# Rotating q through two PSUM banks, k inside the products of v, and a weight split moved behind both

## The chip, the cores and the metric

One Trainium2 chip, one of its cores. The metric is the device time of one launch in microseconds, of which three runs were made of the kernel before: 2287.13, 2292.32 and 2295.41 us, median 2292.32 us. One further execution was recorded by the profiler; everything read from a trace here comes from that one.

## The reference

Two layers of a block for a latent sequence of 512 tokens and a context of 256 tokens, width 1024. Layer 0 mixes with a state-space scan and a long convolution; layer 1 mixes with windowed attention over the latent tokens and the whole context. Each layer has a gated feed-forward network (hidden width 2816). All is float32. The part that the change touches is the start of the attention of layer 1:

```
p = h @ w_qkv                       # q: 16 heads, k and v: 4 heads, 64 wide each
q_l, k_l = axial_rope(q_l), axial_rope(k_l)     # latent tokens only
# per block of 128 queries: scores against 384 neighbours and 256 context keys,
# softmax with a sink, times v; then the output projection
```

`axial_rope` turns each head's columns in pairs: the result is `t * cos + R(t) * sin`, where R swaps the two halves of a group of 32 columns and negates one of them.

## The kernel before, in words

Activations lie transposed, features on the 128 partitions and tokens along the free axis: 768 columns, of which the first 512 are latent. Precision is kept by splitting each operand of a product into a high part and a low part (float32 rounded by a copy, and the rest by a subtraction). Each product is then three matmuls: high weights times high activations, low weights times high, high weights times low (`tiles`, L513, L514, L518).

Weights come in "jobs", each up to 2 x 8 tiles of 128 x 128, in a ring of three slots that SP fills by DMA. A job has two halves, b = 0 and 1. The high part of a half is made by VectorE (`split_high`, L1604, a CAST of 128 x 1024) into `WH`, which has one buffer for each half, and the low part by GpSimd (`low`, L2121) in place. So the split of the next job's half can only begin when TensorE is through with this job's half: `next_high(gs, i, b)` waits on the semaphore `blocks_done` for that. TensorE waits on `w_lo` ahead of each half.

The attention's projections are six jobs, written out in order: jobs 0 to 3 are the eight 128-wide blocks of q (512 columns each), job 4 the two blocks of k (768 columns), job 5 is v (tokens on the partitions: six groups of 24 matmuls of 256 columns, L1052 to L1054; its results lie in PSUM banks 4, 5 and 7, groups 4 and 5 in bank 7). Blocks of q and k accumulate in banks 0 to 3; ScalarE copies each into `T[:, b, :]` (L1473).

The rotation R is one more matmul by a constant matrix, in plain float32 (`rotated(b, n)`, L1036; each makes two records in the trace), from `T[:, b]` into PSUM bank 6. VectorE then makes, for block m, the product of that bank with the sines (L2013), the product of `T[:, b]` with the cosines (L2014) and their sum (L2016), and signals `q_done`. For k (m = 8, 9) it writes the result out into `KD` with four instructions (L2022) and signals `k_done`.

The order on TensorE: block 0 of job n, then the rotations of both blocks of job n - 1, then block 1 of job n. The second of the two rotations waits for `q_done` of the first, because both use bank 6. Both k rotations stand behind v. The order on VectorE: ahead of block m = 2j the splits of both halves for job j + 1, each as `blocks_done` allows; at m = 8 also the splits for the first job of the output projection (`AT["qkv"] + 5` is v, the splits are for the job behind it), which wait for v's last matmuls. Then the ten blocks' arithmetic in order, then `NSINK` (L2027).

Behind that stands the attention itself: scores on TensorE (L1077), which wait for `k_done` and `v_done`; row maxima on VectorE (L2040); exponentials on ScalarE (L1489), with a table load ahead of the first, which also wait for a small copy on GpSimd (L2302) that stands in GpSimd's order behind its splits for the output projection and waits for `NSINK`; transpositions on TensorE (L1089).

Of the kernel before, what the change touches and what calls it, by code (L numbers as in the profile page):

```python
# [7 lines left out]
LAT, CTX = 512, 256  # L8
# [33 lines left out]
IDENT, ONES, KGTJ, KLTJ, LE, GE, ROT = range(7)  # L42


def weight_jobs():

    jobs, at = [], {}

    def stage(name, items):
        at[name] = len(jobs)  # L50
        jobs.extend(items)

    ada0 = [("ada", 0, n) for n in range(24)]
    ada1 = [("ada", 1, n) for n in range(24)]
    stage("ada_a", ada0[:8] + ada1[:8])
    stage("uv", [j for n in range(8) for j in (("uv", 0, n), ada0[8 + 2 * n], ada0[9 + 2 * n])])
    stage("x0", [j for n in range(4) for j in (("x0", 0, n), ada1[8 + 2 * n], ada1[9 + 2 * n])])
    stage("z", [j for n in range(4) for j in (("z", 0, n), ada1[16 + 2 * n], ada1[17 + 2 * n])])
    stage("xbc", [("xbc", 0, n) for n in range(6)])
    stage("out0", [("halves", 0, ((0, 1), (1, 1))), ("halves", 0, ((2, 1), (0, 0))), ("halves", 0, ((1, 0), (2, 0)))])  # L60
    stage("out0b", [("out0", 0, n) for n in range(3, 8)])
    for layer in range(2):
        if layer:
            stage("qkv", [("q", 0, n) for n in range(4)] + [("k", 0, 0), ("v", 0, 0)])
            stage("out1", [("out1", 0, n) for n in range(4)])
        for half in range(2):
            stage(f"up{layer}{half}", [("up", layer, half * FH + n) for n in range(FH)])
            stage(f"down{layer}{half}", [("down", layer, (half, n)) for n in range(8)])
    return jobs, at


JOBS, AT = weight_jobs()
# [90 lines left out]
def build_kernel(nc, A, out):  # L163
    f32 = mybir.dt.float32
    f32r = mybir.dt.float32r
    ALU = mybir.AluOpType
# [3 lines left out]
    with ctx:  # L170
        def sb(name, shape):
            return ctx.enter_context(nc.sbuf_tensor(name, shape, f32))
# [12 lines left out]
        C = sb("consts", [P, 7, P])  # L185
# [36 lines left out]
        T = Tt[:, :].rearrange("p (k t) -> p k t", k=4)  # L222

        def region(at, *dims):

            n = 1
            for d in dims:
                n *= d
            names = "abcd"[:len(dims)]
            ap = R[:, at:at + n]  # L230
            if len(dims) == 1:
                return ap
            return ap.rearrange(f"p ({' '.join(names)}) -> p {' '.join(names)}",
                                **{names[i]: dims[i] for i in range(1, len(dims))})
# [49 lines left out]
        RC = region(8704, 2, LAT)  # L284
# [28 lines left out]
        PS = ctx.enter_context(nc.psum_tensor("psum", [P, 8, 512], f32))  # L313
# [56 lines left out]
        def read(gs, i, b, eng):  # L370

            eng.wait_ge(pair_free[PLAN[gs[0]][b][0]], along([PLAN[g][b][1] + 1 for g in gs], i))
# [115 lines left out]
        def _(pe):  # L488
            mm = pe.matmul

            def half_ready(gs, i, b):
                if JOBS[gs[0]][0] == "ada":
                    pe.wait_ge(w_loaded[gs[0] % SLOTS][b], along([16 * (g // SLOTS + 1) for g in gs], i))
                else:
                    pe.wait_ge(w_lo, along([2 * NTH[g] + b + 1 for g in gs], i))
# [150 lines left out]
            for c in range(2):  # L646

                for t in range(6):
                    n = 6 * c + t
# [27 lines left out]
                for m in range(6):  # L677
                    j, f = 1 - m // 3, m % 3
                    n = 6 * c + m
# [8 lines left out]
                    for odd in range(2):  # L688
                        ts = (2 * odd, 2 * odd + 1) if f < 2 else (4 + odd,)
                        for t in ts:  # L690
                            o = (t * 256 + f * P) if f < 2 else (1024 + (t - 4) * P)
                            ins = mm(PS[:, 2 * (n % 2) + odd, :], C3[:, j, o:o + P], SD[:, j, t, :],  # L692
                                     start=t == ts[0], stop=t == ts[-1])
# [120 lines left out]
            for k in range(KT):  # L814
                for w, moved in ((WDH, HNH0), (WDL, HNH0), (WDH, HNL)):
                    for a, b in SEGS:
                        ins = mm(TP[0:32, a:b], w[:, k, :], moved[:, k, a:b],
                                 start=k == 0 and w is WDH and moved is HNH0, stop=k == KT - 1 and moved is HNL)
            ins.then_inc(dt_mm, 1)
            pe.wait_ge(dt_rows, 1)  # L820
            for t in range(6):
                ins = mm(PS[:, 4, 32 * t:32 * t + 32], T[0:32, 0, t * P:t * P + P], C[0:32, IDENT, 0:32],
                         start=True, stop=True)
# [16 lines left out]
            for n in range(6):  # L840
# [3 lines left out]
                if n == 5:  # L844
# [3 lines left out]
                    for t in range(6):  # L848
                        for q in range(2):
                            ins = mm(NP[32 * q:32 * q + 32, t * P:t * P + P], NAC[:, 32 * t:32 * t + 32], C[:, IDENT, :],  # L850
                                     start=True, stop=True)
# [179 lines left out]
            def rotated(b, n):  # L1031

                read([AT["qkv"] + n // 2], 0, b, pe)
                if n:
                    pe.wait_ge(q_done, n)
                mm(PS[:, 6, :], C[:, ROT, :], T[:, b, 0:LAT], start=True, stop=True).then_inc(q_rot, 1)  # L1036

            for n in range(5):
                two_blocks([AT["qkv"] + n], 0, parts, LS if n < 4 else SEGS,
# [3 lines left out]
            g = AT["qkv"] + 5  # L1043
            half_ready([g], 0, 1)

            for t in range(6):
                acc = PSF[:, 2048 + 256 * t:2048 + 256 * t + 256] if t < 4 else PS[:, 7, 256 * (t - 4):256 * (t - 3)]
                for k in range(KT):
                    wh = WH[:, k // 4, 2 * (k % 4):2 * (k % 4) + 2, :].rearrange("p a b -> p (a b)")
                    wl = WL[:, g % SLOTS, 2 * k:2 * k + 2, :].rearrange("p a b -> p (a b)")  # L1050
                    h, l = HNH[:, k, t * P:t * P + P], HNL[:, k, t * P:t * P + P]
                    mm(acc, h, wh, start=k == 0, stop=False)  # L1052
                    prev = mm(acc, h, wl, start=False, stop=False)
                    ins = mm(acc, l, wh, start=False, stop=k == KT - 1)  # L1054

            prev.then_inc(blocks_done, 1)
            ins.then_inc(blocks_done, 1)
            for b in range(2):
                rotated(b, 8 + b)


            pe.wait_ge(k_done, 2)
            pe.wait_ge(v_done, 2)
# [471 lines left out]
        def _(dve):  # L1535
            ch = Count(dve, v_ch)
            TS, TT, STT = dve.tensor_scalar, dve.tensor_tensor, dve.scalar_tensor_tensor
# [12 lines left out]
            for layer in range(3):  # L1550
                dve.wait_ge(mlp_arg, layer + 1)
                n = 64 if layer < 2 else P
                h, q = HF[layer][0:n, :, :], halves(T[0:n, 0, :], 2)
# [52 lines left out]
            for c in range(2):  # L1606
                for t in range(6):
                    n = 6 * c + t
# [20 lines left out]
                for m in range(6):  # L1629
# [13 lines left out]
                    n = 6 * c + m  # L1643
# [46 lines left out]
            def next_high(gs, i, b):  # L1690

                if gs[-1] + 1 < len(JOBS):
                    dve.wait_ge(blocks_done, along([2 * g + 1 + b for g in gs], i))
                    split_high([SPLIT[NTH[g] + 1] for g in gs], i, b)
# [309 lines left out]
            for m in range(10):  # L2004
                b = m % 2
                if b == 0:
                    for h in range(2):
                        next_high([AT["qkv"] + m // 2], 0, h)
                    if m == 8:
                        for h in range(2):  # L2010
                            next_high([AT["qkv"] + 5], 0, h)
                dve.wait_ge(q_rot, m + 1)
                TT(T[:, 2, 0:LAT], PS[:, 6, :], RC[:, 1, :], ALU.mult)  # L2013
                ch.link(TT(T[:, 3, 0:LAT], T[:, b, 0:LAT], RC[:, 0, :], ALU.mult))  # L2014
                dst = QT[:, m, :] if m < 8 else T[:, b, 0:LAT]
                TT(dst, T[:, 3, 0:LAT], T[:, 2, 0:LAT], ALU.add).then_inc(q_done, 1)  # L2016
                dve.wait_ge(q_done, m + 1)
                if m >= 8:

                    for g in range(2):  # L2020
                        for half in range(2):
                            ins = TS(KD[64 * half:64 * half + 64, 2 * b + g, :],  # L2022
                                     T[64 * g:64 * g + 64, b, :], -1.0, None, ALU.mult)
                    ins.then_inc(k_done, 1)

            dve.wait_ge(v_in, 16)
            TS(NSINK, vec("sink", 0, 16), -1.0, None, ALU.mult).then_inc(at_nsink, 1)  # L2027
# [453 lines left out]
```

## Time and profile before

| | |
|---|---|
| median of three runs | 2292.32 us (2287.13 to 2295.41) |
| profiled execution, its time | 2295.2 us |
| its span, first to last instruction | 2293.4 us |
| mean granted TensorE clock | 0.957 of full speed |
| TensorE matmuls | busy 2127.0 us, 93% of the span, 11802 instructions |
| VectorE | 866.7 us, 38% |
| ScalarE | 439.4 us, 19% |
| GpSimd | 821.3 us, 36% |
| DMA | 182.29 MB, mean 79 GB/s |

"Busy" is the sum of an engine's instruction times. PE is TensorE, PEld its weight loads, DVE VectorE, ACT ScalarE, POOL GpSimd. The granted clock is 1.00 at 2.4 GHz and 0.50 at 1.2 GHz; a value between is a mean over a stretch. The projections of the attention run from about 1578 us to 1697 us of the span, the attention itself from 1711 us to 1844 us.

### The profile page before, as it was taken

What the parts mean: (1) busy time and instruction counts of PE and PEld (TensorE: products, weight loads), DVE (VectorE), ACT (ScalarE), POOL (GpSimd) and SP (SyncE); (2) the same over time, 40 slices, a digit from 0 to 9 for tenths busy, and PEclk for the clock granted to TensorE, in tenths of its full rate; (3) what the DMA queues carried; (4) which work ended last, traced back from release to release, by engine and by line L of the source; (5) the groups of instructions that cost most, each with busy time, mean ns of one, the idle gap of its engine ahead of it and who ended that gap; (6) DMA issues with size and microseconds to landing.
All of it is one profiled execution on the core that took longest, in us unless ns stands there. A gap on an engine that the chain in (4) does not pass through costs nothing.

```text
span 2293.4 us, 29807 instructions
## 1 busy us (share of the span) xinstructions
PE 2127.0 (93%) x11802; PEld 1693.1 (74%) x11802; DVE 866.7 (38%) x1249; ACT 439.4 (19%) x826; POOL 821.3 (36%) x442
## 2 busy tenths in 40 slices
PE   6989988999989978989999999997879998999997
PEld 2468656887877767878888888885656677888886
DVE  4533544302337764241221121233236663322334
ACT  2331110001345541031000011002016612100110
POOL 1443536112227755242222222224210034444442
PEclk9999999999989989989999999998979998999998
DMA  9524323333110011111111211122110021223322
GB/s 340 189 88 165 110 101 112 122 130 115 61 55 2 1 38 57 64 46 65 61 48 63 77 65 62 44 69 75 56 36 1 1 69 65 94 82 105 100 74 73
DMA packets 50838, 182.29 MB, mean 79 GB/s; under 512 B 5680, under 2 KB 5936, under 8 KB 49712
## 3 DMA queue, kind: packets, MB, share of 16 engines
q1 hardware_dynamic: 49296, 171.53, 22.2%
q10 hardware_dynamic: 928, 6.36, 0.8%
q0 software_dynamic: 512, 2.95, 0.4%
q8 instruction: 75, 1.23, 0.2%
q14 instruction: 27, 0.22, 0.0%
HBM read 178.72 MB, written 2.10 MB: 79 GB/s over the span
## 4 chain that ended last, share of the span: by engine, by line
PE 86%; DVE 6%; POOL 3%; ACT 2%; DMA 1%; issue 1%; ACTq 0%; DVEq 0%; SPq 0%
PE psum L513 21%; PE psum L518 21%; PE psum L514 21%; PE psum L1089 2%; PE psum L1077 2%; PE psum L1106 2%; PE psum L692 1%; PE psum L728 1%; PE psum L580 1%; PE psum L655 1%; PE psum L907 1%; POOL weights_lo L2121 1%; PE psum L932 1%; PE psum L536 1%; PE psum L542 1%
## 5 line engine op out<-in xcount | busy, mean ns | idle before, releaser
L2121 POOL TENSOR_TENSOR weights_lo<-weights,weights_hi 128x1024 fp32r<-128x1024 f32 (+1 forms) x232 | 515.1, 2221 | 1034.9 <-DVE weights_hi L1604 1034.9
L1604 DVE CAST weights_hi<-weights 128x1024 fp32r<-128x1024 f32 (+1 forms) x232 | 165.0, 713 | 921.6 <-PE psum L518 751.9
L518 PE MATMUL psum<-normed_lo,weights_hi 128*128 128x512 f32 x1760 | 511.6, 354 | 0.0
L513 PE MATMUL psum<-normed_hi,weights_hi 128*128 128x512 f32 x1088 | 394.8, 363 | 8.4 <-POOL weights_lo L2121 8.4
L514 PE MATMUL psum<-normed_hi,weights_lo 128*128 128x512 f32 x1088 | 376.7, 361 | 0.0
L518 PEld LDWEIGHTS psum<-normed_lo,weights_hi 128*128 128x128 f32 x1760 | 287.2, 191 | 16.8
L513 PEld LDWEIGHTS psum<-normed_hi,weights_hi 128*128 128x128 f32 x1088 | 206.8, 190 | 57.6 <-POOL weights_lo L2121 6.2
L513 PE MATMUL psum<-normed_first_hi,weights_hi 128*128 128x512 f32 (+1 forms) x672 | 234.9, 350 | 13.1 <-POOL weights_lo L2121 12.6
L514 PEld LDWEIGHTS psum<-normed_hi,weights_lo 128*128 128x128 f32 x1088 | 207.7, 191 | 35.5 <-issue 1.2
L514 PE MATMUL psum<-normed_first_hi,weights_lo 128*128 128x512 f32 (+1 forms) x672 | 215.5, 342 | 0.0
L513 PE MATMUL psum<-hidden_hi,weights_hi 128*128 128x512 f32 (+1 forms) x528 | 189.2, 358 | 0.0
L514 PE MATMUL psum<-hidden_hi,weights_lo 128*128 128x512 f32 (+1 forms) x528 | 179.0, 354 | 0.0
L513 PEld LDWEIGHTS psum<-normed_first_hi,weights_hi 128*128 128x128 f32 x672 | 129.3, 192 | 49.7 <-POOL weights_lo L2121 14.6
L518 PE MATMUL psum<-hidden_lo,weights_hi 128*128 128x512 f32 (+1 forms) x528 | 160.5, 358 | 0.0
L514 PEld LDWEIGHTS psum<-normed_first_hi,weights_lo 128*128 128x128 f32 x672 | 129.3, 192 | 16.5 <-issue 1.2
L513 PEld LDWEIGHTS psum<-hidden_hi,weights_hi 128*128 128x128 f32 x528 | 99.1, 188 | 23.4
L514 PEld LDWEIGHTS psum<-hidden_hi,weights_lo 128*128 128x128 f32 x528 | 99.6, 189 | 14.9
L1705 DVE SCALAR_TENSOR_TENSOR temps<-psum,vectors,temps 128x511 f32<-128x511 f32 x112 | 63.8, 612 | 102.6 <-ACT temps L1260 101.6
L1450 ACT ACTIVATE temps<-psum 128x768 f32<-128x768 f32 (+1 forms) x44 | 31.1, 707 | 360.2 <-PE psum L518 355.7
L1454 ACT ACTIVATE hidden_hi<-temps 128x768 f32 (+3 forms) x44 | 32.5, 740 | 334.2 <-DVE temps L1987 334.2
L518 PEld LDWEIGHTS psum<-hidden_lo,weights_hi 128*128 128x128 f32 x528 | 87.1, 188 | 8.9
L513 PE MATMUL psum<-mixed_hi,weights_hi 128*128 128x512 f32 x224 | 77.7, 347 | 8.5 <-POOL weights_lo L2121 8.5
(306 smaller groups left out, 2981.7 us busy)
## 6 DMA issues: line engine op xcount, KB each, us to landing
weights<-in_wall SPq DMA_DIRECT2D x264, 512.0 KB, 4.0
weights<-in_wall SPq DMA_DIRECT2D x32, 384.0 KB, 3.2
weights<-in_wall SPq DMA_DIRECT2D x32, 320.0 KB, 3.1
residual<-in_xT SPq DMA_DIRECT2D x1, 3072.0 KB, 15.4
residual<-in_xT ACTq DMA_DIRECT2D x1, 3072.0 KB, 11.2
phase<-in_tab ACTq DMA_DIRECT2D x2, 1280.0 KB, 5.5
out_T<-normed SPq DMA_DIRECT2D x2, 1024.0 KB, 4.3
normed<-in_window SPq DMA_DIRECT2D x1, 1536.0 KB, 8.7
```

Source lines behind the costliest of these rows:

```text
L513: mm(acc[:, lo:hi], WH[:, b, k, :], high[:, lo:hi], start=st, stop=False)
L514: mm(acc[:, lo:hi], WL[:, s, HALF * b + k, :], high[:, lo:hi], start=False, stop=False)
L518: ins = mm(acc[:, lo:hi], WH[:, b, k, :], low[:, lo:hi], start=False, stop=en)
L536: mm(accs[b][:, lo:hi], WH[:, b, k, :], high[:, lo:hi], start=k == 0, stop=False)
L1077: ins = mm(PSF[:, 1024 * e + at0:1024 * e + at1], QT[rows, 2 * g + j, b * P:b * P + P], KD[rows, g, key:key + at1 - at0], start=c in (0, 2 ...
L1089: ins = pe.transpose(PSF[:, 2048 + t * P:2048 + t * P + P], EX[:, n % 4, 1 + t * P:1 + t * P + P], C[:, IDENT, :])
L1106: ins = mm(PS[64 * e:64 * e + 64, 6, 0:256].rearrange("p (j c) -> p j c", j=2), VT[:, kt, 64 * g:64 * g + 64], heads_e, start=t == 0, stop ...
L1450: run(T[:, 0, lo:hi], pair(0)[:, lo:hi], ACT.Silu).then_inc(pair_free[0], 1)
L1454: run(at_row(HIDH, r)[:, lo:hi], T[:, 1, lo:hi], ACT.Copy).then_inc(hid_hi, 1)
L1604: dve.tensor_copy(WH[:, b, 0:n, :], W[:, s, HALF * b:HALF * b + n, :]).then_inc(w_hi, 1)
L1705: ins = STT(t[:, a:e], p[:, a + shift:e + shift], w, t[:, a:e], ALU.mult, ALU.add)
L2121: TT(WL[:, s, at, :], W[:, s, at, :], WH[:, b, 0:width(gs[0], b), :].bitcast(f32), ALU.subtract).then_inc(w_lo, 1)
```

## The change

Rotations of q (n < 8) go to bank 6 for b = 0 and to bank 7 for b = 1, and rotation n waits for `q_done` n - 1, that is for the block two before it. TensorE waits for `q_done` 8 ahead of v, which writes bank 7. The rotations of k are issued inside v, behind its second and its fourth group of 24 matmuls, and use bank 6. VectorE's two splits for the first job of the output projection move from ahead of block 8's arithmetic to behind block 9's.

```diff
@@ rotated(b, n), TensorE
-                if n:
-                    pe.wait_ge(q_done, n)
-                mm(PS[:, 6, :], C[:, ROT, :], T[:, b, 0:LAT], start=True, stop=True).then_inc(q_rot, 1)
+                if n > 1:
+                    pe.wait_ge(q_done, n - 1 if n < 8 else n)
+                mm(PS[:, 6 + (b if n < 8 else 0), :], C[:, ROT, :], T[:, b, 0:LAT], start=True, stop=True) \
+                    .then_inc(q_rot, 1)
@@ products of v, TensorE
+            pe.wait_ge(q_done, 8)
             for t in range(6):
...
                     ins = mm(acc, l, wh, start=False, stop=k == KT - 1)
+                if t in (1, 3):
+
+                    rotated(t // 2, 8 + t // 2)
 
             prev.then_inc(blocks_done, 1)
             ins.then_inc(blocks_done, 1)
-            for b in range(2):
-                rotated(b, 8 + b)
@@ rotation arithmetic, VectorE
                     for h in range(2):
                         next_high([AT["qkv"] + m // 2], 0, h)
-                    if m == 8:
-                        for h in range(2):
-                            next_high([AT["qkv"] + 5], 0, h)
                 dve.wait_ge(q_rot, m + 1)
-                TT(T[:, 2, 0:LAT], PS[:, 6, :], RC[:, 1, :], ALU.mult)
+                TT(T[:, 2, 0:LAT], PS[:, 6 + (b if m < 8 else 0), :], RC[:, 1, :], ALU.mult)
...
                     ins.then_inc(k_done, 1)
+            for h in range(2):
+                next_high([AT["qkv"] + 5], 0, h)
```

## Rows read from the trace of the kernel before

**Rows 1.** Page, part 4: the chain that ended last, by engine.
```profile
PE 86%; DVE 6%; POOL 3%; ACT 2%; DMA 1%; issue 1%; ACTq 0%; DVEq 0%; SPq 0%
```

**Rows 2.** Waits, 1600 to 1715 us: us in total, times, longest.
```profile
PE psum L1036 <- DVE phase L2016: 8.8, 4, 2.2
```

**Rows 3.** Timeline of TensorE: start us, us, instruction [idle before <-releaser].
```profile
1626.07 1.02 PE L1036 MATMUL psum<-temps,consts 128*128 128x512 f32 x2
...
1637.33 0.40 PE L513 MATMUL psum<-normed_hi,weights_hi 128*128 128x512 f32 x1
...
1642.91 1.02 PE L1036 MATMUL psum<-temps,consts 128*128 128x512 f32 x2
...
1652.64 0.47 PE L513 MATMUL psum<-normed_hi,weights_hi 128*128 128x512 f32 x1
...
1661.08 1.02 PE L1036 MATMUL psum<-temps,consts 128*128 128x512 f32 x2
1664.30 1.52 PE L1036 MATMUL psum<-temps,consts 128*128 128x512 f32 x2 [2.20 <-DVE phase L2016]
...
1678.58 0.58 PE L1052 MATMUL psum<-weights_hi,normed_hi 128*128 128x256 f32 x1 [3.20 <-POOL weights_lo L2121]
```

**Rows 4.** Timelines of VectorE and GpSimd, beside the rotations from 1642.91 us on.
```profile
1643.96 0.69 DVE L2013 TENSOR_TENSOR temps<-psum,phase 128x512 f32<-128x512 f32 x1 [5.74 <-PE psum L1036]
...
1647.33 0.69 DVE L2013 TENSOR_TENSOR temps<-psum,phase 128x512 f32<-128x512 f32 x1 [1.35 <-PE psum L1036]
...
1650.15 2.40 POOL L2121 TENSOR_TENSOR weights_lo<-weights,weights_hi 128x1024 fp32r<-128x1024 f32 x1 [9.45 <-DVE weights_hi L1604]
...
1675.41 0.69 DVE L1604 CAST weights_hi<-weights 128x1024 fp32r<-128x1024 f32 x1 [6.74 <-PE psum L518]
```

**Rows 5.** Chain in order of time: start us, us, what.
```profile
1609.38 0.87 PE psum L1036 x2
```

**Rows 6.** Windows behind waits of TensorE (columns: stretch, length, busy by engine, PEclk, DMA) and two waits.
```profile
1612.40:1617.00 4.60, 4.57 (x12) 3.30 (x13) 2.67 (x4) 0.57 (x1) 0.54 (x1) 0.63 0.03 12
1646.10:1652.60 6.50, 6.47 (x26) 4.82 (x26) 2.67 (x4) 0.57 (x1) 2.40 (x1) 1.00 0.03 11
1026.10:1029.00 2.90, 2.90 (x17) 2.55 (x18) 1.99 (x3) 0.85 (x1) 2.40 (x1) 1.00 0.50 172
1917.30:1921.00 3.70, 3.63 (x9) 2.90 (x10) 2.81 (x3) 0.63 (x1) 2.38 (x1) 0.54 0.41 145
...
1026.06 0.50 PE L513 MATMUL psum<-normed_hi,weights_hi 128*128 128x512 f32 x1 [1.23 <-POOL weights_lo L2121]
...
1917.37 0.77 PE L513 MATMUL psum<-normed_hi,weights_hi 128*128 128x512 f32 x1 [1.91 <-POOL weights_lo L2121]
```

**Rows 7.** Timeline of all engines, end of v to the first transposition.
```profile
1697.21 1.30 DVE L1604 CAST weights_hi<-weights 128x1024 fp32r<-128x1024 f32 x2 [21.10 <-PE psum L1053]
...
1697.98 5.47 POOL L2121 TENSOR_TENSOR weights_lo<-weights,weights_hi 128x1024 fp32r<-128x1024 f32 x2 [19.45 <-DVE weights_hi L1604]
1698.24 0.59 ACT L1479 ACTIVATE phase<-psum 128x512 f32<-128x512 f32 x1
...
1701.29 2.71 DVE L2016 TENSOR_TENSOR temps<-temps 128x512 f32<-128x512 f32 x1
1704.03 2.26 DVE L2022 TENSOR_SCALAR phase<-temps 64x768 f32<-64x768 f32 x4
...
1710.69 2.08 PE L1077 MATMUL psum<-phase 64*128 64x256 f32 x8 [4.50 <-DVE phase L2022]
1710.90 0.19 POOL L2302 COPY phase<-phase 128x4 f32<-128x4 f32 x1 [7.46 <-DVE phase L2027]
1711.17 1.28 ACT L1489 ACT_TABLE_LOAD   x1 [12.33 <-POOL phase L2302]
...
1713.74 0.73 ACT L1489 ACTIVATE phase<-phase 128x513 f32<-128x513 f32 x1 [1.29 <-DVE phase L2040]
...
1716.44 1.11 PE L1089 MATMUL psum<-consts,phase 128*128 128x128 f32 x4
```

## Prediction

> **What bounds the kernel now.** I read the chain that ended last first: 86% of it is TensorE and 6% VectorE [rows 1], so time can only be won where TensorE stands still or runs at its low clock. The waits of the projection stage come next. TensorE stood 8.8 us in front of the rotation matmul, in four waits of 2.2 us each, always for the sum on VectorE [rows 2]. The timelines show the rest: 3.2 us ahead of v for the low part of its weights [rows 3], and from the end of v at 1697.21 us to the first scores at 1710.69 us a stretch of 13.5 us with only the two k rotations on TensorE [rows 7]. The change aims at the four waits and at the long stretch.
>
> **Part 1: two banks for q.** The reader is to follow one period, from one first rotation (time A) to the next. In the third period A is 1642.91 us. The arithmetic of the first block starts at 1643.96, that of the second only at 1647.33 after 1.35 us of idle, then comes the cast, then GpSimd's split from 1650.15 for 2.40 us, and TensorE's next block starts at 1652.64: 9.73 us after A [rows 3, 4]. With bank 7 the second rotation is issued right behind the first. A rotation takes 0.87 us [rows 5], so it ends at A + 1.74, before VectorE is through with the first block (A + 3.1, since the second would have started 1.35 us earlier than A + 4.42). VectorE's idle 1.35 us goes, nearly all of it (I take 1.32), and everything behind it moves up: the next block starts at A + 8.41.
>
> That is not when TensorE is ready. A full block of q takes 1642.91 - 1637.33 = 5.58 us [rows 3], so TensorE is through with two rotations and its block at A + 1.74 + 5.58 = 7.32, and now waits 1.1 us for the split. What is late next is thus the chain of arithmetic, cast and split, and a period is 8.41 + 5.58 = 13.99 us.
>
> - The second period of before lasted 1642.91 - 1626.07 = 16.84 us [rows 3], the first alike (1609.2 to 1626.07). They were longer than the chain asks because the clock fell after the 2.2 us wait: 0.63 in the window behind it [rows 6]. Gain 2.85 us each, 5.7 us.
> - The third kept its clock (1.00 [rows 6]) and was already bound by the split. Gain 9.73 - 8.41 = 1.3 us.
> - The fourth runs from 1661.08 to the end of k's second block, about 1675.2 (0.2 us ahead of the cast it releases at 1675.41 [rows 4]): 14.1 us. k's block takes 1661.08 - 1652.64 = 8.44 us [rows 3], so the new one is 1.74 + 8.44 = 10.2 us. VectorE and GpSimd are done with their part by A + 8.3 and are covered. Gain 3.9 us.
>
> Together 10.9 us. The 3.2 us ahead of v stay: its second half is still cast and split only when k's second block ends. The new wait for `q_done` 8 costs nothing: block 7's sum ends at about A + 5.1, five microseconds before k's second block. The new wait of a rotation for the block two before it has most of a period to spare. Bank 7 holds nothing else then.
>
> **Part 2: k inside v.** v becomes longer by two rotations. No row shows a rotation between matmuls of v; the nearest rows bound one between 0.87 us [rows 5] and 1.52 us at a falling clock [rows 3]. I take 0.87, as v is at full clock by its second group, so 1.7 us are lost. The second rotation waits for the first block's sum. Between them lie 48 matmuls at 18.6 / 144 = 0.13 us (1678.58 to 1697.21 [rows 3, 7]), 6.2 us, and the arithmetic needs 3.1 us, so there is no wait. Behind the second rotation 48 more matmuls follow, 5.6 us or more, plus its own 0.87; VectorE needs 3.1 us and the four writes into `KD`, 2.26 us [rows 7], 5.4 us in all. So `k_done` comes about 1 us ahead of the end of v. If that margin fails, it costs the overrun alone, as v's copies on ScalarE take 1.6 us beyond the end anyway.
>
> **Part 3: the split behind that.** Call the end of v E (1697.21 before). Before, VectorE first made the two casts, and then its sums met GpSimd's splits: the sum at L2016 took 2.71 us [rows 7], where a whole block's three operations otherwise fit into 2 us (A + 1.05 to A + 3.1 above). All this was on the path, 13.5 us to the scores. After, the casts still start at E, since they wait for v, but no k arithmetic follows them. TensorE waits for ScalarE's second copy, which ends at 1698.24 + 0.59, E + 1.6 [rows 7]; the scores start there.
>
> The gain isn't the whole 11.9 us. The exponentials wait for GpSimd's small copy, and this stands behind its two splits. Those start at E + 0.77 and took 5.47 us with VectorE's sums beside them; the split alone takes 2.40 us [rows 4], two 4.8. I take 5.1, because the second cast still overlaps. The copy then ends at E + 6.1, the table load (1.28 us) at E + 7.5, and the first exponential and its sum need 0.9 us [rows 7]; the first transposition starts at E + 8.4. Before, it started at 1716.44, E + 19.2 [rows 7]. Gain 10.8 us. Row maxima and the second pair of scores are ready by then (they took 5.7 us from the first score to that transposition, now E + 7.4), and behind it the order of work is the old one.
>
> The Trainium skill, "SBUF — State Buffer", section "Who interferes with whom", says that a VectorE instruction with two inputs in SBUF shuts GpSimd's reading instructions out or is shut out, whole instructions at a time, and that `tensor_scalar` can be in a mode that does the same. The stretched L2016 agrees. The row maxima have one input in PSUM; the little `NSINK` instruction is a `tensor_scalar`, and gives the rival "lock" below.
>
> **Sum.** 10.9 - 1.7 + 10.8 = 20.0 us off the profiled time of 2295.2 us: 2275.2 us. The median of the runs shown is 2.9 us below the profiled execution (2292.3), so for a median I say 2292.3 - 20.0 = 2272.3 us.
>
> **Rivals.**
> - *The clock falls after the new short waits.* Each 1.1 us wait for the split could do what 2.2 us did in three of four cases. For it: a wait of 1.91 us was followed by 0.54. Against it: 1.23 us by 1.00, and the third 2.2 us wait also by 1.00 [rows 6]. Price of one fall: in the fourth period of before, from the second rotation (1664.30) to the end of k's block (1675.2) went 10.9 us, where 0.87 + 8.44 = 9.3 would do [rows 3], so 1.6 us. Three such waits make 4.8 us: 2277 us. The Trainium skill, "TensorE: Matmul & The Clock Gate", section "A second HAM failure mode: psum-queue depth-cycling", says that cycling through PSUM banks with small pauses makes the clock swing and costs throughput. That is this rival; the trace is on neither side clearly.
> - *Lock.* `NSINK` on VectorE is queued behind the casts and ahead of the row maxima. If it waits until both splits are done (E + 5.9), the maxima follow at E + 6.1, the second pair of scores behind the first of them at E + 7.2, and the transposition 2.7 us later (as from 1713.74 to 1716.44 before [rows 7]) at E + 9.9: 1.5 us lost, 2274 us. Nothing in the rows shows an instruction of 16 columns so held.
> - *The clock is up when the attention starts.* TensorE now pauses 1.6 us instead of 13.5, and might start the attention at its high clock, where the first scores took 2.08 us and the four transpositions 1.11 [rows 7], both at the low one. But it is gated by the exponentials until E + 8.4; at most some 6 us behind that, half paced before, shrink by 3 us (an estimate): 2269 us.
> - *The change doesn't take the stretch away*, because k's arithmetic ends late after all, say v is held for the second rotation by 3 us and `k_done` comes 3 us after E: 6 us less gain, 2278 us. Against it stand the margins of 3 and 1 us above.
> - *Slower.* One mechanism: the clock, once fallen at such a wait, stays at its low level through projections and v. A q block at half pace costs 5.6 us more; the five of them behind the first rotations make 28 us, the two of k at 8.4 more 17 us, and v, 18.6 us before with its start already slow, some 12 more: 57 us against 20 gained, 2329 us. It decides once more than a third of that stretch stays low. Against it: the window of 4.6 us behind a fall has a mean of 0.63 [rows 6], so the clock was up again within it, in the middle of unbroken matmuls, and so it was in the other two falls.
>
> **How the numbers follow.** The forecast as it stands 0.71, clock falls 0.13, lock 0.05, clock up 0.05, not taken away 0.04, slower 0.02. The likeliest gives 2272 us. Upwards the range takes in the clock rival with part of the lock and the scatter of a median (the runs shown lie 8.3 us apart, I allow 3 to 4 us): 2281. Downwards the warm start of the attention and the same scatter: 2264. A measurement of this kernel can tell 0.3%, 6.9 us, from no change; all cases but the last are beyond it on the fast side, yet scatter and some step that I have wrong could eat more: faster 0.95, within 0.3% 0.03, slower 0.02.
>
> **What would show it.** Right: the 2.2 us waits for L2016 gone; in their place three waits of about 1.1 us at L513 for GpSimd's split; periods of 14.0 us; rotations of k inside v, no sum beside a split stretched to 2 us; first score 1.6 us behind v; the table load released by GpSimd's copy about 6 us behind v, the first transposition at 8.4. Wrong: waits of over 2 us at L513, a granted clock of 0.6 behind the short waits, a wait inside v at L1036, or a table load at once behind v, which would mean that GpSimd's copy wasn't what held it.

## The result and the profile after

| | before | after |
|---|---|---|
| median, four runs each | 2289.73 us (2284.95 to 2295.41) | 2267.48 us (2265.93 to 2269.89) |
| profiled execution, its time | 2295.2 us | 2268.76 us |
| its span | 2293.4 us | 2266.9 us |
| mean granted TensorE clock | 0.957 | 0.964 |

The ratio is 0.9902, with a 95% interval of 0.9884 to 0.9919: 22.4 us less, 18.5 to 26.6. A second set of runs (after_again) gave 0.9887 (0.9870 to 0.9903). Forecast were 2272.3 us and a gain of 20.0 us. Of the 4.8 us by which the median came out lower, 2.6 us are the median of before, which a fourth run lowered from 2292.3 to 2289.7 us; the rest is a larger gain.

The first view of the profile after is the timeline of TensorE around the projections, with only the lines that rotate or that stood still. Its columns are those of [rows 3], to which it answers. (Lines moved by one or two: v's first matmul is now L1054, the scores L1079, the transpositions L1091.)

```profile
1603.09 1.88 PE L1036 MATMUL psum<-temps,consts 128*128 128x512 f32 x4
...
1611.46 0.50 PE L513 MATMUL psum<-normed_hi,weights_hi 128*128 128x512 f32 x1 [0.93 <-POOL weights_lo L2122]
...
1617.12 1.88 PE L1036 MATMUL psum<-temps,consts 128*128 128x512 f32 x4
...
1625.49 0.50 PE L513 MATMUL psum<-normed_hi,weights_hi 128*128 128x512 f32 x1 [0.93 <-POOL weights_lo L2122]
...
1631.16 1.88 PE L1036 MATMUL psum<-temps,consts 128*128 128x512 f32 x4
...
1639.53 0.50 PE L513 MATMUL psum<-normed_hi,weights_hi 128*128 128x512 f32 x1 [0.93 <-POOL weights_lo L2122]
...
1648.00 1.88 PE L1036 MATMUL psum<-temps,consts 128*128 128x512 f32 x4
...
1661.47 0.38 PE L1054 MATMUL psum<-weights_hi,normed_hi 128*128 128x256 f32 x1 [3.20 <-POOL weights_lo L2122]
...
1668.77 1.02 PE L1036 MATMUL psum<-temps,consts 128*128 128x512 f32 x2
...
1675.28 1.02 PE L1036 MATMUL psum<-temps,consts 128*128 128x512 f32 x2
```

Both rotations of a pair are now one group of four records, with no wait in front. The first two periods are 14.03 us; the third is 16.84 us, since the block behind its wait is the longer one of k. The k rotations stand inside v, also without a wait. What stands in place of the waits is named in the brackets: 0.93 us for GpSimd's split. The chain in order of time shows who holds whom in one such period: rotation, six operations of VectorE back to back, cast, split.

```profile
1603.25 0.87 PE psum L1036 x2
...
1604.15 0.69 DVE temps L2012
1604.84 0.61 DVE temps L2013
...
1605.47 0.70 DVE phase L2015
...
1606.20 0.69 DVE temps L2012
1606.89 0.61 DVE temps L2013
...
1607.52 0.70 DVE phase L2015
...
1608.25 0.71 DVE weights_hi L1606
...
1609.02 2.39 POOL weights_lo L2122
```

The windows behind the three short waits and over v's start have the columns of [rows 6]; the number to read is the third from the end, the granted clock. It answers to the 0.63 there.

```profile
1611.40:1617.00 5.60, 5.54 (x24) 4.54 (x25) 0.55 (x1) 0.00 (x0) 2.42 (x2) 1.00 0.28 94
1625.40:1631.00 5.60, 5.51 (x24) 4.51 (x25) 0.58 (x1) 0.00 (x0) 2.45 (x2) 1.00 0.30 97
1639.50:1648.00 8.50, 8.47 (x48) 7.43 (x49) 0.52 (x1) 0.00 (x0) 2.42 (x1) 1.00 0.18 62
1661.40:1664.80 3.40, 3.33 (x18) 3.33 (x19) 0.00 (x0) 0.00 (x0) 0.01 (x1) 0.62 0.00 0
```

The timeline of all engines from the end of v on answers to [rows 7].

```profile
1681.87 1.29 DVE L1606 CAST weights_hi<-weights 128x1024 fp32r<-128x1024 f32 x2 [1.21 <-PE psum L1055]
...
1682.64 5.03 POOL L2122 TENSOR_TENSOR weights_lo<-weights,weights_hi 128x1024 fp32r<-128x1024 f32 x2 [21.23 <-DVE weights_hi L1606]
...
1683.08 2.31 DVE L2028 TENSOR_SCALAR phase<-vectors 128x16 f32<-128x16 f32 x1
...
1683.60 1.13 PE L1079 MATMUL psum<-phase 64*128 64x256 f32 x8 [1.65 <-issue]
...
1687.62 0.18 POOL L2303 COPY phase<-phase 128x4 f32<-128x4 f32 x1
...
1687.88 1.28 ACT L1491 ACT_TABLE_LOAD   x1 [4.38 <-POOL phase L2303]
...
1690.05 1.12 PE L1091 MATMUL psum<-consts,phase 128*128 128x128 f32 x4 [1.06 <-ACT phase L1491]
```

The scores follow v by 1.65 us instead of 13.5. The scores aren't the gate any more: ScalarE's table load waits 4.38 us for GpSimd's small copy, which comes as soon as both splits are done, and the first transposition waits for the exponential behind it.

In these two traces the stretch from the first rotation to the first transposition went from 107.23 us (1609.21 to 1716.44) to 86.96 (1603.09 to 1690.05): 20.3 us. From that transposition to the end both need the same, 577.0 and 576.9 us. The rest of the difference between the two spans, 6.1 us, lies ahead of the first rotation, where nothing was changed. I take it for scatter: in the twelve profiles of the experiments the first rotation starts between 1601.8 and 1606.0 us, a range of 4.2 us. The 1609.21 us of the profile of before lie outside even that, so this one execution was unusually late there.

### The profile page after: what moved, and what is told of

Its sections match the earlier page's. It is cut to its first block, busy times and chain, and to the rows that moved or that the text cites. A ratio compares the mean times of both kernels' runs of the same rounds, so it can differ in the third digit from the quotient of the medians.

```text
span 2266.9 us, 29807 instructions
## 1 busy us (share of the span) xinstructions
PE 2113.8 (93%) x11802; PEld 1683.6 (74%) x11802; DVE 867.5 (38%) x1249; ACT 439.3 (19%) x826; POOL 820.2 (36%) x442
## 3 DMA queue, kind: packets, MB, share of 16 engines
q1 hardware_dynamic: 49296, 171.53, 22.4%
## 4 chain that ended last, share of the span: by engine, by line
PE 86%; DVE 6%; POOL 4%; ACT 2%; DMA 1%; issue 1%; ACTq 0%; DVEq 0%; SPq 0%
PE psum L513 21%; PE psum L518 21%; PE psum L514 21%; PE psum L1091 2%; PE psum L1079 2%; PE psum L1108 2%; PE psum L692 1%; POOL weights_lo L2122 1%; PE psum L728 1%; PE psum L580 1%; PE psum L907 1%; PE psum L655 1%; PE psum L932 1%; PE psum L542 1%; PE psum L536 1%
## 5 line engine op out<-in xcount | busy, mean ns | idle before, releaser
L513 PE MATMUL psum<-normed_hi,weights_hi 128*128 128x512 f32 x1088 | 392.5, 361 | 11.4 <-POOL weights_lo L2122 11.4
L513 PEld LDWEIGHTS psum<-normed_hi,weights_hi 128*128 128x128 f32 x1088 | 205.2, 189 | 61.3 <-POOL weights_lo L2122 10.2
L513 PE MATMUL psum<-normed_first_hi,weights_hi 128*128 128x512 f32 (+1 forms) x672 | 234.4, 349 | 13.1 <-POOL weights_lo L2122 12.6
L513 PE MATMUL psum<-hidden_hi,weights_hi 128*128 128x512 f32 (+1 forms) x528 | 189.0, 358 | 0.0
L513 PEld LDWEIGHTS psum<-normed_first_hi,weights_hi 128*128 128x128 f32 x672 | 128.8, 192 | 49.6 <-POOL weights_lo L2122 14.6
L514 PEld LDWEIGHTS psum<-normed_first_hi,weights_lo 128*128 128x128 f32 x672 | 128.8, 192 | 16.6 <-issue 1.2
L513 PEld LDWEIGHTS psum<-hidden_hi,weights_hi 128*128 128x128 f32 x528 | 99.1, 188 | 23.5
L513 PE MATMUL psum<-mixed_hi,weights_hi 128*128 128x512 f32 x224 | 76.8, 343 | 8.5 <-POOL weights_lo L2122 8.5
## 6 DMA issues: line engine op xcount, KB each, us to landing
residual<-in_xT ACTq DMA_DIRECT2D x1, 3072.0 KB, 10.9
```

What stands on the lines that cost most here:

```text
L513: mm(acc[:, lo:hi], WH[:, b, k, :], high[:, lo:hi], start=st, stop=False)
L514: mm(acc[:, lo:hi], WL[:, s, HALF * b + k, :], high[:, lo:hi], start=False, stop=False)
```

## The experiments

Each kernel's stretch from first rotation to first transposition comes from its own profile; that is far finer than the time of a whole run, whose single executions lie up to 12 us apart. The stretch has a scatter too: the same kernel gave 86.96 and 86.85 us, another 76.49 and 77.44. Six kernels were run once only, under the profiler: banks_old_wait (2290.93 us), nsink_early (2268.79), copy_first (2266.89), cast_first (2261.74), v_by_half (2260.68) and longer_wait (2274.90); of those only the stretches are compared. "E" is again the end of v, when the first cast behind it starts.

**q_only: part 1 alone.** The kernel before with these edits:

```diff
-                if n:
-                    pe.wait_ge(q_done, n)
-                mm(PS[:, 6, :], C[:, ROT, :], T[:, b, 0:LAT], start=True, stop=True).then_inc(q_rot, 1)
+                if n > 1:
+                    pe.wait_ge(q_done, n - 1 if n < 8 else n)
+                mm(PS[:, 6 + (b if n < 8 else 0), :], C[:, ROT, :], T[:, b, 0:LAT], start=True, stop=True) \
+                    .then_inc(q_rot, 1)
...
+            pe.wait_ge(q_done, 8)
             for t in range(6):
...
-                TT(T[:, 2, 0:LAT], PS[:, 6, :], RC[:, 1, :], ALU.mult)
+                TT(T[:, 2, 0:LAT], PS[:, 6 + (b if m < 8 else 0), :], RC[:, 1, :], ALU.mult)
```

> The kernel before with part 1 alone: two banks for q and the wait two blocks back; k's rotations behind v and the splits for the output projection where they were. Theory (the parts add up; what is gained is each wait and the clock falls behind it): the stretch from the first rotation to the first transposition falls from 107.2 us by 10.9 to 96.3 us, periods of 14.0, 14.0 and 14.0 us, end of v to first transposition unchanged at 19.2 us; time 0.5% below before. Rival (most of the gain is behind v, the q waits were covered by the split of the weights anyway): the stretch falls by under 5 us.

Measured: stretch 95.74 us, 11.5 less than before; time 0.9946 of before (0.9927 to 0.9966). The first two periods are 14.03 us, and the same three waits of 0.93 us stand at L513. The third is 16.84 us, as in the full change; the 14.0 expected for it overlooked that k's block stands in it. Up to the start of v the gain is 11.0 us (69.37 to 58.38), as in the full change; the other 0.5 us is v, whose low-clock start was shorter in this execution. From E to the first transposition it is 19.22 us, as expected. The rival is out.

**banks_old_wait: the second bank without the new wait.**

```diff
-                mm(PS[:, 6, :], C[:, ROT, :], T[:, b, 0:LAT], start=True, stop=True).then_inc(q_rot, 1)
+                mm(PS[:, 6 + (b if n < 8 else 0), :], C[:, ROT, :], T[:, b, 0:LAT], start=True, stop=True) \
+                    .then_inc(q_rot, 1)
...
+            pe.wait_ge(q_done, 8)
...
-                TT(T[:, 2, 0:LAT], PS[:, 6, :], RC[:, 1, :], ALU.mult)
+                TT(T[:, 2, 0:LAT], PS[:, 6 + (b if m < 8 else 0), :], RC[:, 1, :], ALU.mult)
```

> The kernel before with rotations in banks 6 and 7 but the wait of before (each rotation waits for the sum of the block just ahead of it). Theory: the bank as such changes nothing, the four waits of 2.2 us and the stretch of 107.2 us stay. Rival (cycling through two banks itself moves the clock, for better or worse): waits as before, but the granted clock behind them differs in more than one of the four periods and the stretch by over 2 us.

Measured: stretch 108.64 us. The four waits are there unchanged (the timeline's line of the first is shown), and the windows behind them have a clock of 0.69, 0.69, 0.69 and 0.64: it fell behind all four, where it fell behind three in the kernel before.

```profile
1607.72 2.04 PE L1036 MATMUL psum<-temps,consts 128*128 128x512 f32 x2 [2.20 <-DVE phase L2018]
```

So the bank by itself brings nothing; it is what makes the shorter wait allowed. One further fall in four is less than the "more than one", and 1.4 us of stretch less than the 2 us, that would have spoken for the rival; from one profile no smaller effect of the banks can be ruled out.

**k_and_split: parts 2 and 3 alone.** The changed kernel with bank 6 and the wait of before for q (L2012 reads bank 6 again):

```diff
-                if n > 1:
-                    pe.wait_ge(q_done, n - 1 if n < 8 else n)
-                mm(PS[:, 6 + (b if n < 8 else 0), :], C[:, ROT, :], T[:, b, 0:LAT], start=True, stop=True) \
-                    .then_inc(q_rot, 1)
+                if n:
+                    pe.wait_ge(q_done, n)
+                mm(PS[:, 6, :], C[:, ROT, :], T[:, b, 0:LAT], start=True, stop=True).then_inc(q_rot, 1)
```

> The changed kernel with one bank for q again and the wait of before: parts 2 and 3 alone. Theory: the four waits of 2.2 us are back, the stretch from first rotation to first transposition is 107.2 less 9.1 to 9.4, about 98 us; together with q_only's gain this gives the 20.3 us of the whole. Rival (the parts overlap, because what stands late after one is also late after the other): the two gains add up to 3 us more or less than 20.3.

Measured: stretch 97.96 us, 9.3 less than before; time 0.9941 (0.9920 to 0.9961). With q_only's 11.5 us that makes 20.8, against 20.3 for both together. The parts add up, within the 1 us or so by which one clock fall more or less moves a stretch.

**split_only: the splits moved, k's rotations left behind v.**

```diff
-                    if m == 8:
-                        for h in range(2):
-                            next_high([AT["qkv"] + 5], 0, h)
...
+            for h in range(2):
+                next_high([AT["qkv"] + 5], 0, h)
```

> The kernel before with only the splits for the output projection moved behind the k arithmetic; k's rotations stay behind v. Theory (the exponentials wait for GpSimd's copy behind its splits, so moving the splits behind the arithmetic moves this wait as well): the sums no longer take 2.2 and 2.7 us, the scores start at about 9.7 us behind v instead of 13.5, but the splits start only then, and the first transposition comes at about 18 us instead of 19.2: gain about 1 us. Rival (the contention of VectorE and GpSimd was the price of that stretch): gain 3.5 to 4 us.

Measured: from the first k rotation behind v to the first transposition 17.9 us, where before had 19.3 (1697.12 to 1716.44). The timeline behind that: VectorE's sums are short again, and yet the exponentials start no sooner (17.0 us behind the first k rotation, 16.6 before), since GpSimd's splits now begin at 1704.80, and its small copy and the table load stand behind them.

```profile
1696.66 0.69 DVE L2013 TENSOR_TENSOR temps<-temps 128x512 f32<-128x512 f32 x1
...
1704.05 2.08 PE L1077 MATMUL psum<-phase 64*128 64x256 f32 x8 [4.63 <-DVE phase L2019]
...
1704.80 5.02 POOL L2120 TENSOR_TENSOR weights_lo<-weights,weights_hi 128x1024 fp32r<-128x1024 f32 x2 [30.35 <-DVE weights_hi L1604]
...
1710.03 1.28 ACT L1489 ACT_TABLE_LOAD   x1 [14.04 <-POOL phase L2301]
```

The whole stretch was 107.07 us and the time 0.9990 (0.9979 to 1.0001), no change that can be told. Of the 1.4 us gained here 1.2 were lost again in v, whose first 5.0 us ran at a granted clock of 0.50, where in the kernel before the clock was up again after 3.4 us. So ending the contention of VectorE and GpSimd, 3.6 us of stretched sums, is worth 1.4 us by itself: the splits, and all that waits for GpSimd's copy, then start only behind the sums. With k's arithmetic inside v (k_and_split) the transposition comes at E + 8.18. The other half can't be run alone: with VectorE's splits still ahead of block 8's arithmetic, VectorE waits for the end of v while v waits for block 8's sum ahead of the second rotation, a deadlock by the code. It wasn't tried.

**nsink_early: is the held NSINK a price?** In the changed kernel that instruction of 16 columns took 2.31 us instead of 0.17.

```diff
+            dve.wait_ge(v_in, 16)
+            TS(NSINK, vec("sink", 0, 16), -1.0, None, ALU.mult).then_inc(at_nsink, 1)
             dve.wait_ge(rope_in, 16)
             for m in range(10):
```

> The changed kernel with VectorE's NSINK instruction moved ahead of the ten blocks. In the changed kernel it took 2.31 us instead of 0.17, beside GpSimd's split, and stood ahead of the row maxima. Theory (the first transposition waits for the exponential, and this for GpSimd's copy behind its splits): NSINK takes 0.17 us, the first row maximum comes about 0.7 us earlier, and the first transposition stays at 8.2 us behind v; stretch 87.0 us. Rival (the held instruction delays the maxima and with them the start): the transposition comes 0.7 us or more earlier.

Measured: the first row maximum comes at E + 3.0 instead of 3.6 and the second pair of scores at E + 3.8 instead of 4.4, while the first transposition stays where it was, at E + 8.17 (8.18 in the changed kernel). TensorE only waits longer for the exponential:

```profile
1691.08 0.89 PE L1091 MATMUL psum<-consts,phase 128*128 128x128 f32 x4 [2.55 <-ACT phase L1491]
```

The stretch was 88.09 us, 1.1 more than expected; v was slower by that (21.54 us against 20.40). As the time from E on shows, the held instruction cost nothing.

**copy_first: the gate itself.** As above, and on GpSimd:

```diff
-            for r in range(6):
+            for r in range(5):
                 low([AT["qkv"] + r + 1], 0)
             pool.wait_ge(at_nsink, 1)
+            pool.tensor_copy(MS[:, :, 0], NSINK[:, 0:4]).then_inc(at_sink, 1)
+            low([AT["qkv"] + 6], 0)
...
                 if g:
                     pool.wait_ge(at_exp, 16 * g)
-                pool.tensor_copy(MS[:, :, 0], NSINK[:, 4 * g:4 * g + 4]).then_inc(at_sink, 1)
+                    pool.tensor_copy(MS[:, :, 0], NSINK[:, 4 * g:4 * g + 4]).then_inc(at_sink, 1)
```

> As nsink_early, and GpSimd's small copy stands ahead of its last pair of splits. Theory (that copy is the gate): ScalarE's table load is done during v, the first exponential follows the first row maximum, and the first transposition comes at about 6.5 us behind v instead of 8.2, limited by the second pair of scores; stretch about 85.2 us. Rival (the scores and maxima are the gate): no more than nsink_early.

Measured: stretch 85.07 us. The table load no longer has a wait for GpSimd, and the first transposition starts 5.7 us behind the splits' start (7.4 in the changed kernel), which is E + 6.5:

```profile
1685.30 5.03 POOL L2122 TENSOR_TENSOR weights_lo<-weights,weights_hi 128x1024 fp32r<-128x1024 f32 x2 [20.86 <-DVE weights_hi L1606]
...
1686.17 1.28 ACT L1491 ACT_TABLE_LOAD   x1
...
1688.35 2.74 PE L1079 MATMUL psum<-phase 64*128 64x256 f32 x8 [0.96 <-DVE phase L2041]
...
1691.03 1.11 PE L1091 MATMUL psum<-consts,phase 128*128 128x128 f32 x4
```

GpSimd's copy was the gate, worth 1.7 us (together with the early `NSINK`, which it needs and which alone brought nothing). The other 0.2 us of the stretch is v. One thing differed from the expectation: the table load isn't made during v but behind ScalarE's own copies of v, which stand ahead of it in its order. It is hidden there beside the scores.

**cast_first: what is late next in a q period.**

```diff
+            for h in range(2):
+                next_high([AT["qkv"]], 0, h)
             for m in range(10):
                 b = m % 2
-                if b == 0:
-                    for h in range(2):
-                        next_high([AT["qkv"] + m // 2], 0, h)
+                if b == 0 and m < 8:
+                    next_high([AT["qkv"] + m // 2 + 1], 0, 0)
...
+                if b == 1 and m < 8:
+                    next_high([AT["qkv"] + m // 2 + 1], 0, 1)
```

> The changed kernel with VectorE's cast for the next job's first half ahead of the two rotated blocks instead of behind them. Theory (what is late next in a q period is the chain of arithmetic, cast and split): the three waits of 0.93 us at L513 go, periods of 13.0 to 13.2 us instead of 14.0, and the stretch falls by 2.5 us to 84.5; a sum on VectorE beside the split is held for up to 2 us and hidden. Rival (the held arithmetic now delays ScalarE's copies or the second half's split and gives the time back): periods stay at 13.8 us or more.

Measured: stretch 83.49 us, the first two periods 12.85 us, the third 15.69, no wait at L513 left. This is 1.0 us more gain than expected, and the periods are a little shorter than the 13.0 to 13.2. The price appears where expected, and is hidden: the cosine product beside GpSimd's split takes 2.24 us.

```profile
1602.79 2.39 POOL L2125 TENSOR_TENSOR weights_lo<-weights,weights_hi 128x1024 fp32r<-128x1024 f32 x1 [7.03 <-DVE weights_hi L1606]
1602.87 0.69 DVE L2013 TENSOR_TENSOR temps<-psum,phase 128x512 f32<-128x512 f32 x1 [0.16 <-PE psum L1036]
1603.48 2.24 DVE L2014 TENSOR_TENSOR temps<-temps,phase 128x512 f32<-128x512 f32 x1
1605.76 0.69 DVE L2016 TENSOR_TENSOR phase<-temps 128x512 f32<-128x512 f32 x1
```

The gain of 3.5 us is more than the three waits (2.8 us). The view counts a wait from the end of the last matmul, but matmuls here follow each other every 0.23 us while each lasts 0.40. In the changed kernel the matmul ahead of the first wait started at 1610.13 us and the one behind it at 1611.46, 1.33 us later, so 1.10 us of pace are lost there, and the next one followed only after 0.34 us.

**v_by_half: the 3.2 us ahead of v.**

```diff
-            half_ready([g], 0, 1)
+            half_ready([g], 0, 0)
...
-            for t in range(6):
+            for t, ks in ((0, range(4)), (2, range(4)), (0, range(4, KT)), (1, range(KT)), (2, range(4, KT)),
+                          (3, range(KT)), (4, range(KT)), (5, range(KT))):
...
+                if t == 0 and 4 in ks:
+                    half_ready([g], 0, 1)
```

> The changed kernel with v begun on the first half of its weights: 12 matmuls each of groups 0 and 2 ahead of the wait for the second half. Theory: the wait of 3.2 us ahead of v shrinks to 0.4 us or less, the matmuls keep the high clock, and the stretch falls by 3 to 4 us (2.8 us of wait and the half-paced start of v, 1.7 us) to about 83 us. Rival (the clock falls anyway or the group order costs what it saves): the stretch falls by under 1.5 us.

Measured: stretch 82.48 us, 4.5 less and somewhat more than the 3 to 4 expected. The wait is 0.45 us and the clock stays up, where over the first 3.4 us behind the wait of 3.2 us it was 0.62 (0.52 in the kernel before):

```profile
1657.00:1660.40 3.40, 3.02 (x26) 2.82 (x24) 0.69 (x1) 0.81 (x1) 2.38 (x1) 1.00 0.49 133
1660.40:1676.30 15.90, 15.83 (x124) 14.79 (x124) 8.40 (x14) 0.00 (x0) 0.01 (x1) 1.00 0.02 6
```

**longer_wait: would the new waits have let the clock fall?** Two more products of 0.7 us on VectorE in the second rotated block of each of the first three periods:

```diff
+                if m < 6 and b == 1:
+                    for _ in range(2):
+                        ch.link(TT(T[:, 3, 0:LAT], T[:, b, 0:LAT], RC[:, 0, :], ALU.mult))
```

> The changed kernel with two more products on VectorE (a repeated write of the cosine product, 1.4 us together) in the second rotated block of each of the first three periods, so that the waits at L513 grow from 0.93 to 2.3 us. This asks what the clock would have cost had the new waits been as long as the old. Theory (2.2 us lets the clock fall most times, 0.93 us does not): granted clock of 0.6 behind at least two of the three waits, and the stretch 87 + 3 x 1.4 + 2 or 3 x 1.6, 94 to 96 us. Rival (the banks or the wait's place keep the clock up): 91 us with the clock at 1.00.

Measured: the waits are 2.34 us, the stretch 94.28 us. The windows behind the three waits:

```profile
1614.30:1619.30 5.00, 4.98 (x15) 3.95 (x16) 0.52 (x1) 0.00 (x0) 2.38 (x1) 0.66 0.13 49
1631.30:1636.30 5.00, 4.98 (x15) 3.95 (x16) 0.52 (x1) 0.00 (x0) 2.38 (x1) 0.66 0.16 56
1648.30:1653.30 5.00, 4.98 (x28) 4.38 (x29) 0.52 (x1) 0.00 (x0) 2.42 (x1) 1.00 0.13 50
```

The clock fell behind two of three, and the stretch is within the 94 to 96 us expected. The two periods with a fall are 17.00 us: 14.03 and 1.41 more of wait leave 1.56 us for the fall; the third period grew by 1.47 us alone.

**all_four, after_again, all_four_again: further.** The changed kernel with NSINK early, copy_first, cast_first and v_by_half in one, and beside it the changed kernel again.

> The changed kernel with NSINK early, GpSimd's small copy ahead of its last splits, the cast for the first half ahead of the rotated blocks, and v begun on the first half of its weights. Theory (the three gates stand one behind the other in time and are independent): stretch from first rotation to first transposition 87.0 - 1.7 - 3.5 - 4.0, about 78 us, and the time 9 us (0.4%) below the changed kernel run beside it. Rival (one of them lets the clock fall where it now stays up): stretch 80 us or more.

> The changed kernel once more, beside the version that goes further. Theory: 2268 us, 0.97 to 1.00% below before, stretch 87 to 88 us.

> The version with all four further edits a second time: in its first timing it lay 4.6 us below the changed kernel in the median, where the profiles differ by 10.4 us between first rotation and first transposition. Theory (the stretch is won in full and the rest is scatter outside it): stretch 76 to 78 us, ratio to before 0.985 to 0.987. Rival (the profiled execution was a lucky one, the stretch varies with the clock by several us): stretch 80 us or more, ratio 0.987 to 0.989.

Measured:

| | stretch | median | ratio to before (95%) |
|---|---|---|---|
| after_again | 86.85 us | 2264.80 us | 0.9887 (0.9870 to 0.9903) |
| all_four | 76.49 us | 2260.23 us | 0.9867 (0.9851 to 0.9883) |
| all_four_again | 77.44 us | 2258.94 us | 0.9867 (0.9841 to 0.9892) |

The stretch falls by 9.4 to 10.4 us, close to the sum of the three (1.9 + 3.5 + 4.5 = 9.9). The time falls by less, 4.6 us in the medians of the runs made beside each other, and the two intervals overlap; all four runs of all_four (2254.73 to 2262.18) lie below the four of after_again (2264.28 to 2267.46). The medians of its two sets of runs are 5 to 9 us below the two of the changed kernel; why the whole doesn't show the full 10 is open. The expectations were met in part: all_four's 9 us below after_again came out as 4.6, after_again's gain as 1.13% where 0.97 to 1.00% was expected, and the second timing of all_four lies within its stretch of 76 to 78 us and its ratio of 0.985 to 0.987. The 0.95 us between the two stretches are the clock: the second pair of scores took 1.80 us in one profile and 2.74 in the other. In the two profiles of all_four the part behind the transposition took 571.8 and 576.4 us, a scatter of this size.

## Why the prediction was right

**Part 1, right.** The four waits went and the period became the chain of arithmetic, cast and split: 14.03 us against 13.99 forecast. The wait at L513 reads 0.93 instead of 1.1 us, but that is a matter of counting: the view starts at the end of the last matmul, the forecast at the moment when the next could have started. By that TensorE was ready at A + 7.27 us (7.32 forecast) and lost 1.10 us of pace. The chain, which decides, came out at 8.37 us against 8.41. Gains by period, after against [rows 3]: 2.83, 2.80, 1.33 and, up to the start of v, 4.03; together 11.0 (10.9 forecast). cast_first shows that the chain is the limit, and q_only that the gain is this part's alone.

**The clock, right.** The terms for the first two periods counted a fall behind a wait of 2.2 us as part of what goes, and none behind the new short ones. Over the kernels that have them, the clock fell behind 13 of 16 waits of 2.2 us (before 3 of 4, banks_old_wait 4, split_only 3, k_and_split 3) and behind 2 of 3 of 2.34 us, and behind none of 18 waits of 0.93 us (after, after_again, q_only, nsink_early, copy_first, v_by_half). What the Trainium skill says in "TensorE: Matmul & The Clock Gate", section "A second HAM failure mode: psum-queue depth-cycling", of pauses from cycling through PSUM banks didn't show here at 0.93 us. So the clock rival lay between the two lengths: with VectorE's chain 1.4 us longer it came in (longer_wait).

**Part 2, right.** v took 20.40 us from its first matmul to E, 18.63 before: 1.8 us for two rotations (1.7 forecast), with no wait at either. The second rotation started at 1675.28 us, 3.4 us behind the sum that it waits for, so the rival by which v is held didn't come. Between 1678.39 and 1680.65 us VectorE wrote `KD`, 1.2 us ahead of E.

**Part 3, right, and so was its limit.** The transposition came at E + 8.18 (8.4 forecast), before at E + 19.23: 11.05 us (10.8 forecast). copy_first confirms that GpSimd's copy behind its splits was what kept this from being more, nsink_early that the row maxima weren't.

**Lock, half right and without effect.** I gave it 5% and said that no row shows so small an instruction held. It was held, for 2.31 us, about until the first of the two splits was done and not both. That delayed the maxima by 0.6 us, under the cover of the exponential's wait. This fits what the Trainium skill says of `tensor_scalar` in "SBUF — State Buffer", section "Who interferes with whom"; whether the instruction was in that mode no view shows. The price is nil here.

**Clock up, half right and without effect.** The first eight scores did start at the high clock (granted 1.00 between 1683.6 and 1684.8 us, 1.13 us where before had 2.08). But the second pair took 2.74 us at 0.50 and the first four transpositions 1.12 us at 0.50, about as before, and from the first transposition to the end nothing was gained.

**Slower, out.** No clock stayed low through the projections: behind all three short waits the granted clock was 1.00, and behind the 3.2 us ahead of v it fell, as before, and was up again within v's first group of 24 matmuls.

**The sum.** 11.0 - 1.8 + 11.05 = 20.3 us in the two traces, 20.0 forecast. Over whole runs it was 22.4 us with an interval from 18.5 to 26.6, and 25.9 us (22.2 to 29.8) the second time. The first interval holds 20.3, the second lies above it. Part of that may be luck of the profiled execution of before: one more fall of the clock costs 1.6 us, and banks_old_wait, with the four old waits and the old end, shows a stretch 1.4 us longer. This isn't shown, and where the other few microseconds of the second timing come from wasn't found.

## What to carry to other kernels

Take a period of the critical loop and write down both chains, the one that the change shortens and the one that runs beside it; the gain ends where the second takes over. Here TensorE has to wait for the split in three periods of four, and each such wait is gain that the change doesn't reach. When work moves away from a place, look at what else waits behind it on each queue: GpSimd's four-column copy, behind two splits of 2.4 us, took the gate from the scores. And a wait can have a second price in the clock, which came in at 13 of 16 waits of 2.2 us and at none of 18 of 0.93; so shortening a wait can be worth more than its length.

## What was not expected of the hardware

A VectorE `TENSOR_SCALAR` of 128 x 16 took 2.31 us instead of 0.17 beside a GpSimd subtraction, and a cast of 128 x 1024 issued beside such a split 1.39 us instead of 0.69:

```profile
1610.57 1.39 DVE L1606 CAST weights_hi<-weights 128x1024 fp32r<-128x1024 f32 x1 [1.62 <-PE psum L518]
```

A product of VectorE with one input in PSUM (L2013 in cast_first) took its usual 0.69 us beside a split of the same size. And the clock's falls differ between executions with the same order of instructions on TensorE: behind the 3.2 us wait ahead of v the first matmul took 0.38 us in the changed kernel's profile and 0.58 in nsink_early's, and v took 20.40 and 21.54 us.
